# Attention beside a gate product: probabilities turned in their own step, two steps of them kept

## The chip, the cores and the metric

The kernel runs on 1 core of one Trainium2 chip. The metric is the device time of one execution in microseconds (us). Engines are named as in the profile: PE multiplies matrices, PEld is its weight load, DVE, ACT and POOL are the vector, scalar and general engines, SP issues DMAs. Each engine works through its own instructions in the order written; engines meet only through semaphores.

## The reference, cut to what matters

The program computes two transformer blocks on 512 tokens of width 1024. The second has two attentions, each followed by a gated output projection. The change touches only these two:

```python
# fox_attention: 16 heads, causal, with a decay c added to the logits
logits = einsum('bqhd,bkhd->bhqk', qi, k) * scale + ci[..., :, None] - c_k[..., None, :]
p = softmax(where(causal, logits, -inf))
out = einsum('bhqk,bkhd->bqhd', p, v)
# swa_sink_attention: 16 query heads on 4 key heads, a band of 128 tokens, a sink logit per head
probs = softmax(concatenate([logits, sink]))[..., :-1]
out = einsum('bnhgqk,bnkhd->bqhgd', probs, v_band)
# after either
h = h + (o * silu(gate)) @ w_out        # gate = another 1024 columns of the input projection
```

## The kernel before

The attentions of the second block are written by `attend_beside`, once for each engine, and called with FOX and then SWA. Two heads form a unit `m` (8 units). A unit has four steps `i`, one for each tile of 128 queries, the last tile first; steps are numbered `n = 4m + i`, 0 to 31. In FOX a step sees 512, 384, 256 and 128 keys for i = 0, 1, 2, 3; in SWA 256, 256, 256, 128.

A step goes through this chain: PE computes both heads' scores (`scores_of`, L2087 and the masks L2093, L2104); DVE takes the row maxima (`maxima`, L1308); ACT takes the exponentials into a buffer PBS and their sums (`exps`, L798); DVE inverts the sums (`norms`, L1315); POOL multiplies the probabilities by them, in place (L1691); PE turns them (transposes, `turn_p`, L2124) into two PSUM banks; ACT copies one head's bank to PTS (`turned`, L806), DVE the other's (`turned`, L1321); PE multiplies with the values (`values_of`, L2142).

Beside this PE computes the gate: the transposed gate projection has eight tiles of 128 rows, and one tile is spread over the four steps of a unit, six matmuls of 512 columns in each (`part`, L2167). FOX computes one tile and SWA two ahead of step 0 (`lead`), so units 0 to 6 of FOX and 0 to 5 of SWA have gate products, and the last ones have none. All tiles go through one PSUM bank: `part` of step i = 0 waits for ACT's copy of the tile before (`keep_tile`, L825). The weights of later gate tiles and of the output projection are split into two parts in steps i = 1 and 2 of every second unit (`split`; units 1, 3, 5, 7 of FOX and 0, 2, 4, 6 of SWA; L597, L588 or L594 on ACT, then L1001, L990 or L997 on DVE).

In steps i = 2 and 3 PE also transposes the queries and keys of unit m+2 (`turn`, L2153, in SWA keys only for every second unit, L2156 and L2157), directly ahead of the probabilities and into the same two banks; ACT takes their high part (`high`, L818, which waits for DVE's copy of that step's probabilities), DVE the low part (`low`, L1326). `keep` (L829) takes a unit's output from PSUM. At the end of the attention ACT puts SiLU over the gate tiles (`silu`, L841, L875), and the output projection (L1739) waits for the first gated, split tile (L877, L1356).

The order on each engine is written out by hand. PE's before, for step n: scores of step n+1, values of step n-2, turning of step n-1, gate products of step n. `PBS` has three buffers; the exponentials of step n wait until step n-3 is turned.

Of the kernel before, what the change touches and what calls it, by code (L numbers as in the profile page):

```python
# [211 lines left out]
def program(nc, I, out):  # L212
    RUNS = plan()
    LAST = {a: [g for r in RUNS.values() for g in r if g["by"] == a][-1]["freed"] for a in ("act", "dve")}
    with ExitStack() as ctx:
# [6 lines left out]
        def region(name, where, shape, dt=F32, plus=0):  # L222
            return nc.alloc_sbuf_tensor_at(name, [P, *shape], dt, offset=base + at[where] * KB + plus)
# [4 lines left out]
        def sem(name):  # L228
# [20 lines left out]
              region("pt1", "spl", [2, S], plus=28 * KB)]  # L249
        PTS = [region("pts0", "sc", [2, S], plus=24 * KB), region("pts1", "sc", [2, S])]  # L250
        CK = region("ck", "y", [2, S], BF16, plus=12 * KB)
        PBS = {"fox": [region(f"pbf{i}", "y", [2, S], plus=4 * KB * i) for i in range(3)],
               "swa": [region(f"pbs{i}", "qkv", [2, S], plus=6 * KB + 12 * KB * i) for i in range(3)]}
        C3 = region("c3", "sc", [3, S], BF16, plus=8 * KB)
        CREM = region("crem", "sc", [2, S], plus=12 * KB)
        TS = region("ts", "sc", [2, S], plus=8 * KB)
# [79 lines left out]
        def need(a, k, n):  # L336

            return BESIDE[k], n + (BEFORE[k] if a.is_swa else 0)
# [41 lines left out]
        def score_bank(a, s, h):  # L380

            return 4 * (1 - SIDE[a.name]["group"] % 2) + 2 * (s % 2) + h
# [30 lines left out]
        def reach(eng, s, value):  # L413

            if not (isinstance(value, int) and value <= 0):
                eng.wait_ge(s, value)
# [163 lines left out]
        def _(act):  # L580
# [206 lines left out]
            def attend_beside(a):  # L787

                s, g = A[a.name], SIDE[a.name]

                def exps(n):
                    m, i = divmod(n, NT)
                    t = NT - 1 - i
                    reach(act, *need(a, "pt_tr", n - 2))
                    w = a.width(t) + a.sink
                    for h in range(2):
                        act.wait_ge(*need(a, "mx", 2 * n + h + 1))
                        last = act.activation(PBS[a.name][n % 3][:, h, 0:w], PS[:, score_bank(a, n, h), 0:w], ACT.Exp,  # L798
                                              bias=NM[:, m % 2, h, t:t + 1], accum_out=LS[:, m % 2, h, t:t + 1])
                    last.then_inc(s["e"], 1)  # L800

                def turned(n):
                    w = a.width(NT - 1 - n % NT)
                    act.wait_ge(*need(a, "pt_tr", n + 1))
                    reach(act, *need(a, "v", n - 1))
                    act.activation(PTS[0][:, n % 2, 0:w], PS[:, turn_bank(a, PT_BANK), 0:w], ACT.Copy)\  # L806
                       .then_inc(s["pt_a"], 1)

                def high(m, i):
                    if i:  # L810
                        act.wait_ge(*need(a, "tk", a.keys_of(m) + 1))
                    else:
                        act.wait_ge(*need(a, "tq", m + 1))
                    if m >= 2:
                        act.wait_ge(*need(a, "s", 8 * (m - 1)))
                        act.wait_ge(*need(a, "pt_b", NT * (m - 2) + 3 + i))
                    slot = (a.keys_of(m) if i else m) % 2
                    act.activation(turned_to(m, slot, i, HI), turned_at(a, m, i), ACT.Copy).then_inc(s["th"], 1)  # L818

                def keep_tile(k):  # L820
                    if k % 2:
                        act.wait_ge(unit_used, g["unit"] + k // 2 + 1)
                    else:
                        act.wait_ge(*need(a, "tile", k // 2 + 1))
                    act.activation(MX[:, k], PS[:, turn_bank(a, SIDE_BANK)], ACT.Copy).then_inc(s["kept"], 1)  # L825

                def keep(m):
                    act.wait_ge(*need(a, "v", NT * (m + 1)))
                    act.activation(kept_output(m), by_tile(PS[:, turn_bank(a, PV_BANK)]), ACT.Copy)\  # L829
                       .then_inc(s["o"], 1)  # L830

                def split(m, part):
                    if a.split_at(m) is None:
                        return
                    n = g["unit"] + a.split_at(m)
                    act.wait_ge(raw_full[n % 2], 16 * (n // 2 + 1))
                    act.wait_ge(unit_used, n - 1)
                    side_hi(n, part)

                def silu(k):  # L840
                    act.activation(MX[:, k], MX[:, k], ACT.Silu).then_inc(s["silu"], 1)  # L841

                if a.is_fox:
                    act.wait_ge(cum_out, 16)
                    act.wait_ge(x_parked, 16)
                for m, i in a.first_turns():
                    high(m, i)
                for k in range(a.lead):
                    keep_tile(k)
                exps(0)  # L850
                for n in range(a.steps + 2):
                    m, i = divmod(n, NT)
                    if i == 0 and a.tile_at(m - 1) is not None:
                        keep_tile(a.tile_at(m - 1))
                    if n + 1 < a.steps:
                        exps(n + 1)
                    if i == 1 and m:
                        keep(m - 1)
                    if 1 <= n <= a.steps:
                        turned(n - 1)  # L860
                        if a.turn_with(n - 1):
                            high(*a.turn_with(n - 1))
                    if n >= a.steps - 1:
                        silu(2 * (n - a.steps + 1))
                        silu(2 * (n - a.steps + 1) + 1)
                    if i in (1, 2):
                        split(m, i - 1)
            def gated_hi(a):
# [116 lines left out]
        def _(dve):  # L985
# [307 lines left out]
            def attend_beside(a):  # L1293
# [40 lines left out]
                    low(m, i)  # L1334
                maxima(0)
                norms(0)
                for n in range(a.steps + 1):
                    m, i = divmod(n, NT)
                    if n + 1 < a.steps:
                        maxima(n + 1)  # L1340
                    if n >= 1:
                        turned(n - 1)
                    if n + 1 < a.steps:
                        norms(n + 1)
                    if n >= 1 and a.turn_with(n - 1):
                        low(*a.turn_with(n - 1))
                    if i in (1, 2):
                        split(m, i - 1)

# [212 lines left out]
        def _(pool):  # L1562
# [116 lines left out]
            def attend_beside(a):  # L1679
                s = A[a.name]  # L1680
                if a.is_fox:
                    pool.wait_ge(x_parked, 16)
                    pool.memset(CK[:], 0.0).then_inc(ck_zero, 1)
                for n in range(a.steps):
                    m, i = divmod(n, NT)
                    t = NT - 1 - i
                    w = a.width(t)
                    pool.wait_ge(*need(a, "r", n + 1))
                    for h in range(2):
                        p = PBS[a.name][n % 3][:, h, 0:w]  # L1690
                        last = pool.tensor_tensor(p, p, RR[:, m % 2, h, t:t + 1].to_broadcast([P, w]), ALU.mult)  # L1691
                    last.then_inc(s["scaled"], 1)

# [36 lines left out]
        def _(pe):  # L1730
# [339 lines left out]
            def attend_beside(a):  # L2070
# [38 lines left out]
                def turn_p(n):  # L2109
                    t = NT - 1 - n % NT  # L2110
                    pe.wait_ge(*need(a, "scaled", n + 1))
                    reach(pe, *need(a, "pt_a", n))
                    reach(pe, *need(a, "pt_b", n))
                    if n and a.turn_with(n - 1):
                        before, i = a.turn_with(n - 1)
                        if i:
                            pe.wait_ge(*need(a, "kt", a.keys_of(before) + 1))
                        else:
                            pe.wait_ge(*need(a, "qt", before + 1))
                    if a.turn_with(n):  # L2120
                        turn(*a.turn_with(n))
                    for h in range(2):
                        for i in range(a.width(t) // P):
                            last = pe.transpose(PS[:, turn_bank(a, PT_BANK + h), P * i:P * i + P],  # L2124
                                                PBS[a.name][n % 3][:, h, P * i:P * i + P], IDF[:])
                    last.then_inc(s["pt_tr"], 1)

                def values_of(n):
# [61 lines left out]
                pe.wait_ge(freed["act"], last_in[-1]["freed"])  # L2190
                pe.wait_ge(consts, 14)
                scores_of(0)
                for n in range(a.steps + 2):
                    m, i = divmod(n, NT)
                    if n + 1 < a.steps:
                        scores_of(n + 1)
                    if n >= 2:
                        values_of(n - 2)
                    if 1 <= n <= a.steps:
                        turn_p(n - 1)  # L2200
                    part(m, i)

            norm_x(0, None)
            run(RUNS["diff_in"])
# [73 lines left out]
```

## Time and profile before

| | |
|---|---|
| median of three runs | 1901.98 us (1901.42 to 1902.23) |
| profiled execution, its own time | 1901.54 us |
| its span | 1899.7 us |
| PE busy | 1742.6 us (92% of the span) |
| FOX: first scores to the first product of its output projection | 1437.39 to 1566.85 us |
| SWA: the same | 1717.76 to 1846.86 us |
| PE busy in these two stretches | 120.64 of 129.55 us, 109.57 of 129.16 us |

The two attentions take 259 us together. The rest of the program is not touched. A matmul's end is modelled in the profile: the next one starts some 0.1 to 0.3 us ahead of it, so PE's own pace is read from start to start.

### The profile page before, as it was taken

Reading aid. Unit: us, or ns where it says so; the run is one execution under the profiler, and the core shown is the slowest. Engines: PE = TensorE matmul, PEld = TensorE weight load, DVE = VectorE, ACT = ScalarE, POOL = GpSimd, SP = SyncE. Lnnn points to the kernel's source line nnn. Section 1 sums busy time; section 2 is a strip of 40 time slices with the busy share of each in tenths; the row PEclk is TensorE's granted clock in tenths of the full one; section 3 lists DMA queues with packets and bytes.
Section 4 is the critical chain, followed back from the end, with each engine's and each line's share of the span. In section 5 each row is a group of like instructions: output and inputs, shape, how many; then the busy total and the mean of one; then the engine's idle time right before and its main releaser. Section 6 shows DMA issues by size and latency. Waiting matters only on the chain.

```text
span 1899.7 us, 24666 instructions
## 1 busy us (share of the span) xinstructions
PE 1742.6 (92%) x9327; PEld 1354.8 (71%) x9327; DVE 894.4 (47%) x1582; ACT 718.4 (38%) x1568; POOL 367.0 (19%) x498
## 2 busy tenths in 40 slices
PE   6999788999978998998999999989998989888978
PEld 5888557868664554886888888867786767676656
DVE  3782473225445666344343244244644554455552
ACT  3322464122135666323332133133224562434451
POOL 5440242002114564011000000000102330022220
PEclk9999796999987999999999999989999999899979
DMA  6223121422102221432222322332221013220101
GB/s 174 86 92 122 50 73 56 133 89 89 45 12 56 67 58 32 155 104 96 66 90 89 110 89 96 104 111 77 87 82 45 24 36 120 67 89 24 45 23 45
DMA packets 117779, 147.64 MB, mean 78 GB/s; under 512 B 30685, under 2 KB 63733, under 8 KB 117425
## 3 DMA queue, kind: packets, MB, share of 16 engines
q1 hardware_dynamic: 116608, 145.40, 24.0%
q0 software_dynamic: 992, 0.86, 0.4%
q8 instruction: 68, 1.11, 0.2%
q14 instruction: 31, 0.25, 0.0%
q10 hardware_dynamic: 80, 0.02, 0.0%
HBM read 125.24 MB, written 4.24 MB: 68 GB/s over the span
## 4 chain that ended last, share of the span: by engine, by line
PE 81%; ACT 8%; DVE 7%; issue 3%; POOL 1%; DMA 0%; ACTq 0%; DVEq 0%; POOLq 0%
PE ps L1739 57%; PE ps L2167 4%; PE ps L1978 3%; PE ps L2002 2%; ACT pb L740 2%; PE ps L2124 2%; PE ps L2142 2%; PE ps L2087 1%; PE ps L2021 1%; PE ps L2035 1%; DVE qkt L1241 1%; DVE nm L1211 1%; ACT qkt L759 1%; PE ps L1983 1%; PE ps L1876 1%
## 5 line engine op out<-in xcount | busy, mean ns | idle before, releaser
L1739 PE MATMUL ps<-spl,ht 128*128 128x512 f32 x2496 | 584.3, 397 | 26.5 <-DVE xk L1465 8.5
L1739 PEld LDWEIGHTS ps<-spl,ht 128*128 128x128 f32 x2496 | 478.8, 192 | 129.6 <-DVE xk L1465 9.0
L1022 DVE TENSOR_TENSOR spl<-raw,spl 128x1024 fp32r<-128x1024 f32 x180 | 234.7, 1346 | 521.9 <-ACT spl L620 521.9
L620 ACT ACTIVATE spl<-raw 128x1024 fp32r<-128x1024 f32 x180 | 180.5, 1052 | 598.7 <-PE ps L1739 598.7
L1739 PE MATMUL ps<-ht,spl 128*128 128x512 f32 x1152 | 263.9, 391 | 2.0 <-DVE spl L1022 2.0
L1739 PEld LDWEIGHTS ps<-ht,spl 128*128 128x128 f32 x1152 | 217.6, 189 | 48.1 <-issue 2.9
L1739 PE MATMUL ps<-spl,uu 128*128 128x512 f32 x768 | 174.4, 389 | 0.0
L1739 PEld LDWEIGHTS ps<-spl,uu 128*128 128x128 f32 x768 | 144.2, 188 | 29.9
L1636 POOL TENSOR_TENSOR sq<-qkv 128x2048 f32<-128x2048 f32 (+1 forms) x15 | 51.5, 3436 | 372.2 <-ACT qkv L654 357.6
L2167 PE MATMUL ps<-ht,spl 128*128 128x512 f32 x384 | 108.9, 425 | 10.5 <-DVE qkt L1326 5.4
L740 ACT ACTIVATE pb<-ps,nm 128x512 f32<-128x512 f32 (+1 forms) x192 | 99.8, 530 | 45.5 <-DVE nm L1211 45.4
L1672 POOL TENSOR_TENSOR pb<-pb,rg 128x512 f32<-128x512 f32 (+3 forms) x160 | 112.8, 722 | 7.5
L1211 DVE TENSOR_REDUCE nm<-ps 128x1 f32<-128x512 f32 (+1 forms) x192 | 85.2, 485 | 54.4 <-PE ps L1983 54.2
L2167 PEld LDWEIGHTS ps<-ht,spl 128*128 128x128 f32 x384 | 72.6, 201 | 24.8 <-DVE qkt L1326 5.7
L1739 PE MATMUL ps<-ys,spl 128*128 128x512 f32 x384 | 89.2, 395 | 0.0
L1697 POOL MEMSET nws<- 128x2048 f32 x2 | 3.6, 1807 | 440.5 <-PE ps L1739 440.5
L1739 PEld LDWEIGHTS ps<-ys,spl 128*128 128x128 f32 x384 | 73.3, 191 | 15.6 <-issue 0.2
L1978 PE MATMUL ps<-qkt 64*128 64x384 f32 (+3 forms) x576 | 77.4, 377 | 7.2 <-DVE qkt L1241 3.0
L2002 PEld LDWEIGHTS ps<-idf,pb 128*128 128x128 f32 x400 | 44.9, 143 | 36.2 <-issue 29.1
L1691 POOL TENSOR_TENSOR pbf<-pbf,rr 128x512 f32<-128x512 f32 (+3 forms) x64 | 44.7, 721 | 133.6 <-DVE rr L1315 133.6
L1978 PEld LDWEIGHTS ps<-qkt 64*128 64x128 f32 x576 | 47.7, 204 | 28.2 <-issue 23.5
L1308 DVE TENSOR_REDUCE nm<-ps 128x1 f32<-128x257 f32 (+5 forms) x128 | 53.3, 437 | 30.3 <-PE ps L2104 27.7
(292 smaller groups left out, 2060.8 us busy)
## 6 DMA issues: line engine op xcount, KB each, us to landing
raw<-w_in SPq DMA_DIRECT2D x30, 1024.0 KB, 5.2
raw<-w_mlp_up SPq DMA_DIRECT2D x16, 1024.0 KB, 5.2
raw<-w_mlp_down SPq DMA_DIRECT2D x16, 1024.0 KB, 5.0
raw<-w_in_a SPq DMA_DIRECT2D x16, 1024.0 KB, 5.3
stq<-qkv SPq DMA_DIRECT2D x32, 256.0 KB, 2.7
raw<-w_in_b SPq DMA_DIRECT2D x8, 1024.0 KB, 5.4
raw<-w_proj_diff SPq DMA_DIRECT2D x4, 1024.0 KB, 5.2
stq<-qkv SPq DMA_DIRECT2D x32, 128.0 KB, 2.5
```

The lines of the kernel that those rows point to most:

```text
L620: act.activation(SPL[:, n % 2, HI, 2 * k:2 * k + 2], RAW[:, n % 2, 2 * k:2 * k + 2], ACT.Copy).then_inc(hi_done, 1)
L740: last = act.activation(p, PS[:, 2 * (idx % 2) + h, 0:w], ACT.Exp, bias=NM[:, m.slot, h, t:t + 1], accum_out=LS[:, m.slot, h, t:t + 1])
L1022: dve.tensor_tensor(SPL[:, n % 2, LO, 2 * k:2 * k + 2], RAW[:, n % 2, 2 * k:2 * k + 2], SPL[:, n % 2, HI, 2 * k:2 * k + 2].bitcast(F32), A ...
L1211: dve.tensor_reduce(top, bank[:, 0:w], AX.X, ALU.max, negate=True).then_inc(s["mx"], 1)
L1308: dve.tensor_reduce(NM[:, m % 2, h, t:t + 1], bank[:, 0:w + a.sink], AX.X, ALU.max, negate=True)\
L1636: pool.tensor_tensor(SQ[:, :, 0:w], QKV[:, :, col:col + w], QKV[:, :, col:col + w], ALU.mult)\
L1672: last = pool.tensor_tensor(p, p, RG[:, m.slot, h, t:t + 1].to_broadcast([P, w]), ALU.mult)
L1691: last = pool.tensor_tensor(p, p, RR[:, m % 2, h, t:t + 1].to_broadcast([P, w]), ALU.mult)
L1739: last = pe.matmul(PS[:, b0 + b], left[:, x], right[:, y], start=(kt == 0 and i == 0), stop=(kt == UK * g["units"] - 1 and i == 2))
L1978: pe.matmul(PS[:, 2 * (idx % 2) + h, 0:w], QKT[r, m.slot, 0, x, P * t:P * t + P], QKT[r, m.slot, 1, y, P * a.first_key(t):P * t + P], star ...
L2002: last = pe.transpose(bank[:, P * i:P * i + P], PB[:, m.slot, h, o:o + P], IDF[:])
L2167: last = pe.matmul(PS[:, turn_bank(a, SIDE_BANK)], wide(SPL[:, n % 2, x])[:, kt, cols], HT[:, y, kt], start=(kt == 0 and j == 0), stop=(kt ...
```

## The change

Turning moves from the step after into the step itself, behind the gate products, and the value products from two steps after into the next one. There is one closing step less. PBS has two buffers. On ACT and DVE the copies move with the turning; `keep` moves from i = 1 to i = 0, and the SiLUs begin one step number earlier.

```diff
-        PBS = {"fox": [region(f"pbf{i}", "y", [2, S], plus=4 * KB * i) for i in range(3)],
-               "swa": [region(f"pbs{i}", "qkv", [2, S], plus=6 * KB + 12 * KB * i) for i in range(3)]}
+        PBS = {"fox": [region(f"pbf{i}", "y", [2, S], plus=4 * KB * i) for i in range(2)],
+               "swa": [region(f"pbs{i}", "qkv", [2, S], plus=6 * KB + 12 * KB * i) for i in range(2)]}
...
 ACT, exps(n)
-                    reach(act, *need(a, "pt_tr", n - 2))
+                    reach(act, *need(a, "pt_tr", n - 1))
 ACT, loop
-                for n in range(a.steps + 2):
+                for n in range(a.steps + 1):
...
                     if n + 1 < a.steps:
                         exps(n + 1)
-                    if i == 1 and m:
+                    if i == 0 and m:
                         keep(m - 1)
-                    if 1 <= n <= a.steps:
-                        turned(n - 1)
-                        if a.turn_with(n - 1):
-                            high(*a.turn_with(n - 1))
-                    if n >= a.steps - 1:
-                        silu(2 * (n - a.steps + 1))
-                        silu(2 * (n - a.steps + 1) + 1)
+                    if n < a.steps:
+                        turned(n)
+                        if a.turn_with(n):
+                            high(*a.turn_with(n))
+                    if n >= a.steps - 2:
+                        silu(2 * (n - a.steps + 2))
+                        silu(2 * (n - a.steps + 2) + 1)
                     if i in (1, 2):
                         split(m, i - 1)
 DVE, loop
-                for n in range(a.steps + 1):
+                for n in range(a.steps):
...
                         maxima(n + 1)
-                    if n >= 1:
-                        turned(n - 1)
                     if n + 1 < a.steps:
                         norms(n + 1)
-                    if n >= 1 and a.turn_with(n - 1):
-                        low(*a.turn_with(n - 1))
+                    turned(n)
+                    if a.turn_with(n):
+                        low(*a.turn_with(n))
                     if i in (1, 2):
                         split(m, i - 1)
 PE, loop
-                for n in range(a.steps + 2):
+                for n in range(a.steps + 1):
...
                         scores_of(n + 1)
-                    if n >= 2:
-                        values_of(n - 2)
-                    if 1 <= n <= a.steps:
-                        turn_p(n - 1)
+                    if n >= 1:
+                        values_of(n - 1)
                     part(m, i)
+                    if n < a.steps:
+                        turn_p(n)
```

PE in the middle of FOX before, two steps (i = 0 and i = 1 of a unit; pbf is PBS, pts PTS, spl with ht the gate products), as far as the second step's value product, of which the first two rows stand:

```order
L2087 MATMUL ps<-qkt 128x256 x6
L2093 MATMUL ps<-ck,oneb 128x256 x2
L2104 MATMUL ps<-causal,id 128x128 x4
L2142 MATMUL ps<-pts_68,qkv 64x128
L2142 MATMUL ps<-pts_69,qkv 64x128
L2124 MATMUL ps<-idf,pbf_73 128x128 x8
L2167 MATMUL ps<-ht,spl 128x512 x6
L2087 MATMUL ps<-qkt 128x128 x6
L2093 MATMUL ps<-ck,oneb 128x128 x2
L2104 MATMUL ps<-causal,id 128x128 x4
L2142 MATMUL ps<-pts_68,qkv 64x128
L2142 MATMUL ps<-pts_69,qkv 64x128
```

The same place after the change, from the first step's gate products on (lines are one lower throughout):

```order
L2166 MATMUL ps<-ht,spl 128x512 x6
L2123 MATMUL ps<-idf,pbf_71 128x128 x8
L2086 MATMUL ps<-qkt 128x256 x6
L2092 MATMUL ps<-ck,oneb 128x256 x2
L2103 MATMUL ps<-causal,id 128x128 x4
L2141 MATMUL ps<-pts_68,qkv 64x128
L2141 MATMUL ps<-pts_69,qkv 64x128
```

The eight transposes of a 512-key step (x8) stood ahead of the gate products; now they stand behind them, and only the next step's scores stand between them and their own value product.

ACT at the end of FOX before (L588 is the second half of a weight split, L841 SiLU, mx the gate tiles):

```order
L798 ACTIVATE pbf_72,ls<-ps,nm 128x128 x2
L806 ACTIVATE pts_68<-ps 128x384
L588 ACTIVATE spl<-raw 128x1024
L806 ACTIVATE pts_68<-ps 128x256
L841 ACT_TABLE_LOAD
L841 ACTIVATE mx<-mx 128x512 x2
L806 ACTIVATE pts_68<-ps 128x128
```

And after the change:

```order
L798 ACTIVATE pbf_72,ls<-ps,nm 128x128 x2
L806 ACTIVATE pts_68<-ps 128x256
L841 ACT_TABLE_LOAD
L841 ACTIVATE mx<-mx 128x512 x2
L588 ACTIVATE spl<-raw 128x1024
L806 ACTIVATE pts_68<-ps 128x128
```

The table load and the first two SiLUs stood behind the second half of the split; now they stand ahead of it.

## Rows read from the trace of the kernel before

**Rows 1.** Windows: us, busy time (instructions) by engine, granted PE clock, DMA share, GB/s

```profile
1469.00:1485.00 16.00, 16.00 (x143) 12.00 (x142) 7.55 (x19) 8.58 (x28) 5.73 (x9) 1.00 0.17 63
1762.00:1769.00 7.00, 4.52 (x44) 3.36 (x44) 4.14 (x13) 4.56 (x15) 1.83 (x4) 1.00 0.25 69
1769.00:1776.00 7.00, 6.72 (x20) 3.80 (x20) 2.18 (x8) 1.91 (x6) 1.30 (x3) 0.53 0.22 83
```

**Rows 2.** Groups by line, PE, 1437 to 1566.8: busy us, mean ns, idle before, releasers

```profile
L2142 PE MATMUL ps<-pts,qkv 128*64 128x128 f32 x320 | 25.4, 289 | 3.9 <-ACT pts L806 3.3 <-DVE pts L1321 0.6
```

**Rows 3.** The same for PE, 1717 to 1846.8

```profile
L2142 PE MATMUL ps<-pts,qkv 128*64 128x128 f32 x224 | 21.2, 308 | 12.5 <-ACT pts L806 11.2 <-DVE pts L1321 1.2
```

**Rows 4.** PE's timeline, steps of a middle unit of FOX: start, us, instructions [idle before]

```profile
1489.26 0.62 PE L2087 MATMUL ps<-qkt 64*128 64x256 f32 x6
...
1490.05 0.44 PE L2142 MATMUL ps<-pts,qkv 128*64 128x128 f32 x4
1490.42 1.09 PE L2124 MATMUL ps<-idf,pbf 128*128 128x128 f32 x8
1491.27 1.64 PE L2167 MATMUL ps<-ht,spl 128*128 128x512 f32 x6
1492.84 0.55 PE L2087 MATMUL ps<-qkt 64*128 64x128 f32 x6
...
1493.51 1.09 PE L2142 MATMUL ps<-pts,qkv 128*64 128x128 f32 x16
1494.53 0.88 PE L2124 MATMUL ps<-idf,pbf 128*128 128x128 f32 x6
1495.16 1.63 PE L2167 MATMUL ps<-ht,spl 128*128 128x512 f32 x6
1496.72 0.96 PE L2087 MATMUL ps<-qkt 64*128 64x512 f32 x6
...
1497.96 0.88 PE L2142 MATMUL ps<-pts,qkv 128*64 128x128 f32 x12
```

**Rows 5.** DVE's timeline, the same stretch

```profile
1491.55 0.69 DVE L1321 COPY pts<-ps 128x512 f32<-128x512 f32 x1 [0.64 <-PE ps L2124]
...
1497.34 1.22 DVE L1001 TENSOR_TENSOR spl<-raw,spl 128x1024 fp32r<-128x1024 f32 x1 [1.16 <-ACT spl L597]
1498.48 1.28 DVE L1308 TENSOR_REDUCE nm<-ps 128x1 f32<-128x512 f32 x2
```

**Rows 6.** PE's timeline, start and end of FOX

```profile
1443.28 1.09 PE L2124 MATMUL ps<-idf,pbf 128*128 128x128 f32 x8 [1.31 <-POOL pbf L1691]
...
1559.94 1.12 PE L2142 MATMUL ps<-pts,qkv 128*64 128x128 f32 x8 [0.61 <-DVE pts L1321]
...
1566.85 33.48 PE L1739 MATMUL ps<-spl,ht 128*128 128x512 f32 x137 [3.72 <-DVE ht L1356]
```

**Rows 7.** DVE's timeline, end of FOX

```profile
1559.37 0.42 DVE L1321 COPY pts<-ps 128x256 f32<-128x256 f32 x1
```

**Rows 8.** ACT's timeline, the middle unit of FOX

```profile
1496.24 1.06 ACT L597 ACTIVATE spl<-raw 128x1024 fp32r<-128x1024 f32 x1
1499.26 0.69 ACT L798 ACTIVATE pbf<-ps,nm 128x512 f32<-128x512 f32 x1 [1.95 <-DVE nm L1308]
...
1500.86 0.60 ACT L818 ACTIVATE qkt<-ps 128x512 fp32r<-128x512 f32 x1
1501.34 0.62 ACT L825 ACTIVATE mx<-ps 128x512 f32<-128x512 f32 x1
```

**Rows 9.** POOL's timeline, the middle unit of FOX

```profile
1500.98 2.04 POOL L1691 TENSOR_TENSOR pbf<-pbf,rr 128x512 f32<-128x512 f32 x2 [3.97 <-DVE rr L1315]
```

**Rows 10.** ACT's timeline, end of FOX

```profile
1559.77 1.28 ACT L841 ACT_TABLE_LOAD   x1
1561.07 1.15 ACT L841 ACTIVATE mx<-mx 128x512 f32<-128x512 f32 x2
```

**Rows 11.** PE's timeline, unit 2 of SWA

```profile
1769.28 0.27 PE L2156 MATMUL ps<-idf,qkv 128*64 128x128 f32 x1 [0.65 <-DVE qkt L1326]
```

More of the change, by code:

```diff
@@ L797, in exps @@
                         act.wait_ge(*need(a, "mx", 2 * n + h + 1))
-                        last = act.activation(PBS[a.name][n % 3][:, h, 0:w], PS[:, score_bank(a, n, h), 0:w], ACT.Exp,
+                        last = act.activation(PBS[a.name][n % 2][:, h, 0:w], PS[:, score_bank(a, n, h), 0:w], ACT.Exp,
                                               bias=NM[:, m % 2, h, t:t + 1], accum_out=LS[:, m % 2, h, t:t + 1])
@@ L1689, in attend_beside @@
                     for h in range(2):
-                        p = PBS[a.name][n % 3][:, h, 0:w]
+                        p = PBS[a.name][n % 2][:, h, 0:w]
                         last = pool.tensor_tensor(p, p, RR[:, m % 2, h, t:t + 1].to_broadcast([P, w]), ALU.mult)
@@ L2124, in turn_p @@
                             last = pe.transpose(PS[:, turn_bank(a, PT_BANK + h), P * i:P * i + P],
-                                                PBS[a.name][n % 3][:, h, P * i:P * i + P], IDF[:])
+                                                PBS[a.name][n % 2][:, h, P * i:P * i + P], IDF[:])
                     last.then_inc(s["pt_tr"], 1)
```

## The prediction

> **What bounds the kernel now.** I read the windows first, then PE's timeline with what it waits for, then DVE's, ACT's and POOL's over the same microseconds. In the middle of FOX PE is busy for all of 16.00 us at full clock while DVE and ACT work for about half of that and POOL for a third [rows 1]. So there PE's own work sets the pace, and the softmax chain lies wholly under it. At the end of FOX the gate products have run out, and the value products wait for the copies of the turned probabilities: 3.9 us in all, all of it behind the last gate products [rows 2]. In SWA the steps are shorter and the same kind of wait comes to 12.5 us [rows 3]; after such waits (PE busy for 4.52 of 7.00 us) the granted clock fell to 0.53 for the next 7 us, so at 1.2 GHz for nearly all of it [rows 1]. The question is therefore not whether the change takes work from PE (it takes none: the same matmuls) but whether each wait that it brings is still hidden.
>
> **PE's paces.** From start to start [rows 4]: scores of 256 keys 0.79 (1489.26 to 1490.05), of 128 keys 0.67, of 512 keys 1.24; values of 128 keys 0.37, of 512 keys 1.02; the turning of 512 keys 0.85, of 384 keys 0.63; a step's gate products 1.57. For what is not in the rows I interpolate by blocks: scores of 384 keys 1.02, values of 384 and 256 keys 0.81 and 0.59, turning of 256 and 128 keys 0.41 and 0.20, turning four query blocks 0.49. A turning's end lies 0.24 behind the start of what follows (1490.42 + 1.09 against 1491.27), and the copies begin 0.04 after that end [rows 4, 5]. A DVE copy of 512 keys lasts 0.69 [rows 5]; of 256 keys 0.42, and PE went on 0.15 after it ended (1559.37 + 0.42 to 1559.94) [rows 6, 7].
>
> **Two buffers instead of three.** The exponentials of step n+1 now need step n-1 turned. Their scores stand behind that turning on PE, take 0.67 or more, and a maximum follows; the turning is reported 0.28 after PE goes on. Price 0. Without that cover, it would cost the 0.28.
>
> **The wider gap that is left for the softmax.** For a 512-key step the chain is: DVE's first maximum to ACT's first exponential 0.78 (1498.48 to 1499.26) [rows 5, 8], exponential to POOL 1.72, POOL 2.04 [rows 8, 9], and 0.16 for the two ends: 4.7 us after the scores. PE now has between scores and turning: values 0.59, gate 1.57, turns 0.49 + 0.20, scores 1.02, values 0.37, gate 1.57: 5.8 us. Hidden, with 1.1 to spare. At the start there is less in between: before, PE waited 1.31 shown with the scores of step 2 already issued [rows 6]; now these 0.77 us stand behind the wait. **Plus 0.8.**
>
> **The copies lose their cover.** Before, gate products and scores (1.57 and 0.67 to 1.24) lay between a turning and its value product. Now only the scores do. For 512 keys the copy is usable at 0.24 + 0.04 + 0.69 + 0.15 = 1.12 after PE goes on; the scores behind it (256 keys) take 0.78. PE stands 0.34. For 384 keys (copy estimated 0.56) it is 0.99 against 0.67: 0.32. Behind the two narrow steps stand scores of 512 and 384 keys, long enough. That is 0.66 in each of units 0 to 6: **plus 4.6**.
>
> **The gate tile's bank.** The first gate products of a unit wait for ACT's copy of the tile before. ACT's queue now has ahead of it the copy and the high part of the last step, which come after the gate products instead of before them. From the end of the last turning: DVE's copy 0.04 to 0.33, high part until its queue time of 0.48 is over (1500.86 to 1501.34 [rows 8]) at 0.86, the tile's copy 0.62 [rows 8] and 0.05: 1.53. PE arrives at -0.24 + 1.02 + 0.37 = 1.15. **0.38** for units 2, 4, 6 and, with the split's lateness below, 0.66 for units 3, 5, 7's tiles: **plus 3.1**.
>
> **The splits.** In step i = 2 ACT makes its half behind the copy and the high part, and DVE's next maxima stand behind DVE's half. Before this made the maxima start 0.4 late, hidden [rows 5]. Now both halves wait for a turning that comes after the gate products. From the end of that turning: ACT's copy, high part behind DVE's copy, over at 1.0; split 1.06 to 2.05 [rows 8]; DVE's 1.14 (1497.34 to 1498.48 [rows 5]) until 3.2; first exponential at 4.0, both done at 5.4; then DVE inverts and copies the last step's probabilities, usable at 6.0. PE is there at -0.24 + 1.24 + 0.59 + 1.57 + 0.49 + 0.20 + 1.02 = 4.9. So 1.1 in units 1, 3 and 5: **plus 3.4**.
>
> **The end of FOX.** There is one step less, but no gate product covers anything, a split lies in it (unit 7), and its second half now stands on ACT behind the table load and two SiLUs, as the order shows. By the same sums PE waits 0.9, 0.34 and 0.32 in steps 28 to 30 of PE's order, 2.5 for the copy of step 30 (behind DVE's first split half and the last maxima), and for the last copy: from DVE's previous copy, ACT's table load 1.28 and two SiLUs (1.04 of ACT's queue) [rows 10], its split 1.06, DVE's split 1.2, the copy and 0.15: 3.7 of it uncovered. Sum 7.8. The same sum for before gives 5.7, of which the rows show 3.9 as idle behind the modelled ends [rows 2]. **Plus 2.1.** What follows the last value product (keep, SiLUs, first gated tile) is the same chain as before, with its wait of 3.72 [rows 6].
>
> Here the Trainium skill (ScalarE: Activation LUTs, What ACT_TABLE_LOAD costs) has a higher price than the row: a table load of about 1283 ns and a drain of about 1380 ns for each change of set. The row shows 1.28 us and the first SiLU 0.02 later (1559.77 + 1.28 to 1561.07) [rows 10], so no drain behind it; by the page the last term would be 1.4 larger, by the row it stands.
>
> **FOX together**: 0.8 + 4.6 + 3.1 + 3.4 + 2.1 = **14.0**; I take 13.8, since ACT is a little less behind at the very end.
>
> **SWA.** Its scores are shorter (0.66 and 0.61) and steps narrower. The same sums, laid out step by step, give lateness up to unit 5: before 10.9 (the first steps 1.75; at the splits of units 0 and 2 1.6 + 1.5 + 0.7 and 1.4 + 1.5 + 0.7; unit 4 1.5). After: 2.4 at the start, 1.1 of copies in each of units 1, 3 and 5, 3.1 in units 0 and 2 (0.2, 0.25, 1.35, 0.6, 0.7), 1.4 in unit 4: 13.3. Plus 2.4. The wait of 0.65 ahead of the keys' turning [rows 11] vanishes, since gate products stand in between; that is in the sum. In the last two units, with no gate products: 11.0 before and 10.4 after, one step less: minus 0.6, and another 0.6 less because the short end spends less work at the low clock. Then the clock: before, it fell in unit 2 when waits of that unit came close together. Seven microseconds at 0.53 with 6.72 busy hold work of about 4 us at full clock: some 2.7 lost [rows 1]. After the change the waits there are spread over more places (the largest is 1.35), so I take it that it stays up: minus 2.7. **SWA: 2.4 - 0.6 - 0.6 - 2.7 = -1.5.**
>
> **Sum**: 13.8 - 1.5 = 12.3 us. The sum is made against the profiled execution's 1901.54, which lies 0.4 under the median: 1913.8, or 1914.3 against the median. I say **1914**.
>
> **Rivals.**
> 1. *The clock falls in more places* (14%). For it: in SWA it fell after 4.52 busy of 7.00. Against it: unit 0 had nearly the same waits without a fall, and in FOX's split units I get about a quarter idle. If it falls in three FOX units and in both SWA splits, five falls at 2.7 instead of one: +13.5 - 2.7 over the forecast's none, 1914 + 11 = 1925 or so. The Trainium skill (TensorE: Matmul & The Clock Gate, A second HAM failure mode: psum-queue depth-cycling) describes such a kernel: short idles between groups of matmuls, often enough, make the clock swing. The trace shows one such fall, at 1769, and none in the first split unit.
> 2. *Copies are in time* (17%). If a value product can follow a copy sooner than the 0.15 at the end suggests, or ACT's and DVE's queues run earlier than I lay them, then the 4.6 and most of the 3.1 vanish: 1914 - 7 = 1907. Decides: whether the copy of 512 keys is usable within 0.78.
> 3. *Faster* (5%). The closing step is all that counts. Between the last value products before, 2.7 us each at the end of FOX (1557.3 to 1559.9) and as much in SWA; with both gone, the fall at 1769 avoided (2.7) and the keys' wait (0.65 in three units) hidden, 1902 - 10 = 1892; with a part of the copies' waits, 1897. It decides if no wait stands in units 1 to 6 of FOX.
> 4. *No change* (4%): 2 and 3 cancel, 1902.
>
> **How the numbers follow.** Forecast 60%, its own range 1908 to 1921: each of some forty waits is good to 0.1 or 0.2, one fall of the clock may come or go. Faster by over 0.2% (3.8 us, about what a measurement of this kernel tells from no change): rival 3, 0.05. Same: rival 4, 0.04. Slower: 0.91. The range takes in rival 2 and most of the way to rival 1: 1905 to 1923.
>
> **What would show it.** In FOX's middle PE's timeline should show value products with waits of about 0.1 shown (0.34 less the modelled drain of 0.24) released by DVE's pts, waits for mx (L825) at each unit's first gate product, and a unit of 16.7 us without and 18.2 with a split instead of 15.7. At FOX's end a wait of over 3 us ahead of the last value product, with ACT's table load and SiLUs ahead of the split. FOX's stretch should be 143 us instead of 129.6, SWA's 127 to 129. The prediction is wrong if FOX's middle shows PE without waits, if PE waits for POOL's pbf in every step (a chain longer than 5.8), or if the clock falls in FOX's middle.

## The result: 1911.9 against 1901.7 us, 0.6% slower

| | before | changed |
|---|---|---|
| median | 1901.7 us (4 runs, 1899.9 to 1902.23) | 1911.88 us (4 runs, 1911.18 to 1914.52) |
| ratio | | 1.0058, 95% interval 1.0040 to 1.0075 |
| profiled execution, span | 1901.54, 1899.7 us | 1912.05, 1910.2 us |
| FOX: first scores to the first product of its projection | 129.46 us | 141.19 us |
| between FOX and SWA | 150.91 us | 149.83 us |
| SWA: the same | 129.10 us | 128.58 us |

The prediction was 1914, range 1905 to 1923. The loss lies wholly in FOX (+11.7 us); SWA came out 0.5 us shorter, and the stretch between, whose code is the same, 1.1 us shorter.

PE's timeline of the changed kernel in FOX, from the first gate product of unit 1 to that of unit 2 (columns as in [rows 4]; unit 1 has the splits):

```profile
1458.62 1.65 PE L2166 MATMUL ps<-ht,spl 128*128 128x512 f32 x6 [0.22 <-ACT mx L825]
1460.12 1.04 PE L2123 MATMUL ps<-idf,pbf 128*128 128x128 f32 x8
1461.08 0.62 PE L2086 MATMUL ps<-qkt 64*128 64x256 f32 x6
...
1461.98 1.09 PE L2141 MATMUL ps<-pts,qkv 128*64 128x128 f32 x16
...
1464.50 0.82 PE L2123 MATMUL ps<-idf,pbf 128*128 128x128 f32 x6
1465.26 0.55 PE L2086 MATMUL ps<-qkt 64*128 64x128 f32 x6
...
1466.07 0.88 PE L2141 MATMUL ps<-pts,qkv 128*64 128x128 f32 x12
...
1475.47 0.44 PE L2141 MATMUL ps<-pts,qkv 128*64 128x128 f32 x4 [1.00 <-DVE pts L1321]
1476.58 1.66 PE L2166 MATMUL ps<-ht,spl 128*128 128x512 f32 x6 [0.67 <-ACT mx L825]
```

Two kinds of wait are flagged, for the gate tile's copy (mx) and, in a unit with splits, for the last step's copy (pts). A third is not shown as idle: from the turning of 512 keys to its value product there are 1.86 us (1460.12 to 1461.98) where turning and scores alone took 0.85 + 0.79 before [rows 4]. The modelled ends of the matmuls cover it.

DVE's and ACT's timelines of the same unit show the chain behind the wait of 1.00:

```profile
1461.19 0.69 DVE L1321 COPY pts<-ps 128x512 f32<-128x512 f32 x1 [0.39 <-PE ps L2123]
...
1469.44 0.43 DVE L1321 COPY pts<-ps 128x256 f32<-128x256 f32 x1
1470.61 0.69 DVE L1326 TENSOR_TENSOR qkt<-ps,qkt 128x512 fp32r<-128x512 f32 x1 [0.74 <-ACT qkt L818]
1471.56 1.23 DVE L1001 TENSOR_TENSOR spl<-raw,spl 128x1024 fp32r<-128x1024 f32 x1 [0.25 <-ACT spl L597]
1472.70 1.28 DVE L1308 TENSOR_REDUCE nm<-ps 128x1 f32<-128x512 f32 x2
1474.96 0.17 DVE L1315 RECIPROCAL rr<-ls 128x2 f32<-128x2 f32 x1 [0.97 <-ACT pbf L798]
1475.04 0.29 DVE L1321 COPY pts<-ps 128x128 f32<-128x128 f32 x1
```

```profile
1469.98 0.60 ACT L818 ACTIVATE qkt<-ps 128x512 fp32r<-128x512 f32 x1 [0.16 <-DVE pts L1321]
1470.48 1.05 ACT L597 ACTIVATE spl<-raw 128x1024 fp32r<-128x1024 f32 x1
1473.48 0.69 ACT L798 ACTIVATE pbf<-ps,nm 128x512 f32<-128x512 f32 x1 [1.95 <-PE ps L2123]
```

In the order of the steps: the copy of step 2 releases ACT's high part, that its split, that DVE's split; only then come the maxima of the next unit (1472.70; its scores were issued at 1469.33), their exponentials, and behind these on DVE the copy of step 3 (1475.04), for which PE stands.

The end of FOX in the changed kernel, PE and then ACT:

```profile
1570.01 0.66 PE L2141 MATMUL ps<-pts,qkv 128*64 128x128 f32 x8 [2.31 <-DVE pts L1321]
1570.59 0.44 PE L2123 MATMUL ps<-idf,pbf 128*128 128x128 f32 x2
1574.61 0.69 PE L2141 MATMUL ps<-pts,qkv 128*64 128x128 f32 x4 [3.58 <-DVE pts L1321]
```

```profile
1569.62 1.28 ACT L841 ACT_TABLE_LOAD   x1
1570.91 1.15 ACT L841 ACTIVATE mx<-mx 128x512 f32<-128x512 f32 x2
1571.97 1.04 ACT L588 ACTIVATE spl<-raw 128x1024 fp32r<-128x1024 f32 x1
```

DVE in the same place:

```profile
1573.04 1.23 DVE L990 TENSOR_TENSOR spl<-raw,spl 128x1024 fp32r<-128x1024 f32 x1 [3.18 <-ACT spl L588]
1574.18 0.28 DVE L1321 COPY pts<-ps 128x128 f32<-128x128 f32 x1
```

The last copy on DVE waits behind DVE's half of the split, and that behind ACT's, which now comes after the table load and two SiLUs.

By groups of lines (busy us, mean ns, idle before, releasers), PE from 1437.6 to 1578.8 (FOX) of the changed kernel:

```profile
L2166 PE MATMUL ps<-ht,spl 128*128 128x512 f32 x169 | 46.9, 411 | 2.7 <-ACT mx L825 2.7
L2141 PE MATMUL ps<-pts,qkv 128*64 128x128 f32 x320 | 24.8, 283 | 9.8 <-DVE pts L1321 8.9
...
L2123 PE MATMUL ps<-idf,pbf 128*128 128x128 f32 x160 | 23.0, 274 | 3.0 <-POOL pbf L1690 3.0
```

The value products' waits went from 3.9 [rows 2] to 9.8 us, almost all for DVE's copy.

Where FOX's time lies can be read without the modelled ends, from the start of one group of scores to that of another. Unit 0 is here from the scores of step 1 to those of step 5, units 1 to 6 from there to the scores of step 29, the end from there to the projection; the 1.1 us ahead of step 1's scores are the same in all. The lower four kernels are those of the experiments below.

| | unit 0 | units 1 to 6 | end | FOX |
|---|---|---|---|---|
| before | 15.54 | 93.83 | 18.97 | 129.46 |
| changed | 18.14 | 102.39 | 19.53 | 141.19 |
| SiLUs behind the split | 18.11 | 102.48 | 18.25 | 139.95 |
| splits ahead of the copies | 18.13 | 99.81 | 19.09 | 138.15 |
| both repairs | 18.10 | 97.88 | 19.09 | 136.19 |
| turned ahead of the gate products | 21.52 | 98.64 | 19.59 | 140.87 |

At the scores of step 5 the changed order has done one turning and one value product more than the order of before, about 1.3 us by its rows; that work is moved from the end into unit 0. Put back, the changed kernel's 11.7 us are about 1.3 at the start, 8.6 in the middle and 1.9 at the end (an estimate from the table).

### The profile page after: what moved, and what is told of

It is laid out like the page before. It is cut to its first block, busy times and chain, and to the rows that moved or that the text cites. A ratio compares the mean times of both kernels' runs of the same rounds, so it can differ in the third digit from the quotient of the medians.

```text
span 1910.2 us, 24667 instructions
## 1 busy us (share of the span) xinstructions
PE 1745.2 (91%) x9327; PEld 1359.7 (71%) x9327; DVE 896.2 (47%) x1582; ACT 722.3 (38%) x1568; POOL 366.7 (19%) x498
## 4 chain that ended last, share of the span: by engine, by line
PE 80%; ACT 9%; DVE 7%; issue 3%; POOL 1%; DMA 0%; ACTq 0%; DVEq 0%; POOLq 0%
PE ps L1738 57%; PE ps L2166 4%; PE ps L1977 3%; PE ps L2001 2%; ACT pb L740 2%; PE ps L2141 2%; PE ps L2123 2%; PE ps L2020 1%; PE ps L2086 1%; PE ps L2034 1%; DVE qkt L1241 1%; DVE nm L1211 1%; PE ps L1982 1%; ACT qkt L759 1%; PE ps L1875 1%
## 5 line engine op out<-in xcount | busy, mean ns | idle before, releaser
L1738 PEld LDWEIGHTS ps<-ys,spl 128*128 128x128 f32 x384 | 73.5, 192 | 15.7 <-issue 0.2
L2001 PE MATMUL ps<-idf,pb 128*128 128x128 f32 x400 | 64.2, 285 | 0.0
```

What stands on the lines that cost most here:

```text
L1738: last = pe.matmul(PS[:, b0 + b], left[:, x], right[:, y], start=(kt == 0 and i == 0), stop=(kt == UK * g["units"] - 1 and i == 2))
L2001: last = pe.transpose(bank[:, P * i:P * i + P], PB[:, m.slot, h, o:o + P], IDF[:])
```

## The experiments

Stretches are from one profiled execution of each; times are medians of the runs named. The edits are shown against the changed kernel, unless said otherwise.

### Three buffers in the new order

```diff
-        PBS = {"fox": [... for i in range(2)], "swa": [... for i in range(2)]}
+        PBS = {"fox": [... for i in range(3)], "swa": [... for i in range(3)]}
-                    reach(act, *need(a, "pt_tr", n - 1))
+                    reach(act, *need(a, "pt_tr", n - 2))
```
(and the buffer's number `n % 3` instead of `n % 2` on ACT, POOL and PE)

> The changed kernel's order with three probability buffers instead of two, in both attentions. Theory A (the order costs: copies, gate tile's bank, splits, end of FOX): nothing comes back, since the exponentials' scores stand behind the turning on PE; FOX's stretch stays at 141.2 us within 0.5, the time at 1912 within 2. Rival B (the missing third buffer costs): FOX's stretch falls towards 129.5 us and the time towards 1902; anything under 1908 speaks for it. Rival C (falls of the clock cost): no change either, but the cost then has to lie in stretches at 1.2 GHz.

FOX took 141.20 us (141.19 with two), SWA 128.61 (128.58). The one run's 1909.0 us differs through what lies ahead of FOX: there the first scores came at 1434.67 us, in the changed kernel at 1437.69, from the same code. So in the new order the third buffer is worth nothing, and rival B falls. The time missed the expected 1912 within 2 by 1.0 us, for that reason.

### Two buffers in the old order

```diff
-                    reach(act, *need(a, "pt_tr", n - 2))
+                    reach(act, *need(a, "pt_tr", n - 1))
```
(in the kernel before, and both lists with two buffers)

> The order of before, with two probability buffers. Here the turning of step n-1 stands in the same step of PE as the scores of step n+1 and behind them, so the exponentials of n+1 wait for it: their start moves from 0.8 us behind the scores to the end of values and turning, 1 to 2 us. Theory A: by the sums of the prediction this is not hidden at the splits of FOX and in SWA: FOX 129.5 plus 4 to 7, SWA plus 2 to 5, time 1907 to 1913. Rival B as the whole cause would give the same here as the changed kernel, 1912, and a FOX stretch of 141. If the buffers cost nothing in any order: 1902.

1910.3 us (one run), FOX 134.22 and SWA 132.94. The old order needs the third buffer: its absence costs FOX 4.8 us, and in every unit of the middle (16.3 to 16.4 us instead of 15.7), not only at the splits as expected. The new one doesn't need it, and costs 11.7 for other reasons. The two halves of the change can't be priced apart and added.

### SWA alone, FOX alone

```diff
         self.lead, self.run, self.steps = lead, run, NT * units
+        self.back = int(name not in ('swa',))
```
(for the second, 'fox'; where `back` is 1, the loops, the offsets and the number of buffers are as before the change)

> SWA in the new order with two buffers, FOX as before with three. Theory A: FOX's stretch 129.5, SWA's 127 to 130 (in the changed kernel 128.6 against 129.1), time 1899 to 1903. Rival C (the clock decides): a fall of the clock more or less in SWA moves this by 2.7 us either way. If SWA carries a real part of the loss, the time is over 1904.

> FOX in the new order with two buffers, SWA as before with three. Theory A: FOX's stretch 141.2, SWA's 129.1, time 1901.7 plus 10 to 12, 1911 to 1914, nearly the whole loss. If the two attentions share the loss: about 1907.

SWA alone: 1899.1 us (10 runs, 1896.2 to 1904.0) against 1901.2 of before on the same chip, ratio 0.9991 (0.9982 to 1.0001): no difference that can be told. Its SWA stretch was 125.95 us, under the expected 127 to 130. FOX alone: 1908.5 us (6 runs), under the expected 1911 to 1914, ratio 1.0035 (1.0022 to 1.0048), with a FOX stretch of 141.16 as in the changed kernel. So the loss is FOX's. In the profiled execution it is +11.7 in FOX, -1.1 between the two and -3.6 in SWA, which took 125.51 us against 129.10 with the same code as before. That the other five runs are short for the same reason is likely, but they have no trace.

What made SWA shorter is the clock. In unit 2 both executions have the same waits, of 1.36 and 0.65 us. First the kernel before (the wait of 0.65 is in [rows 11]), then this one:

```profile
1767.97 0.66 PE L2142 MATMUL ps<-pts,qkv 128*64 128x128 f32 x8 [1.36 <-ACT pts L806]
...
1769.48 0.69 PE L2157 MATMUL ps<-idf,qkv 128*64 128x128 f32 x2
```

```profile
1780.32 0.66 PE L2147 MATMUL ps<-pts,qkv 128*64 128x128 f32 x8 [1.36 <-ACT pts L807]
1781.62 0.27 PE L2161 MATMUL ps<-idf,qkv 128*64 128x128 f32 x1 [0.65 <-DVE qkt L1328]
1781.82 0.43 PE L2162 MATMUL ps<-idf,qkv 128*64 128x128 f32 x2
```

Behind them the same two transposes take 0.69 us in one and 0.43 in the other: in one execution the clock fell to 1.2 GHz, in the other it stayed at 2.4. The second had its own fall earlier, 20 us after SWA's first scores, and hardly one in the last two units, where before ran some 12 us at the low clock. The fall in unit 2 cost the kernel before 2.8 us (20.57 from the scores of step 13 to those of step 17, against 17.74). The earlier one cost FOX alone 1.5, and its end, from the scores of step 29, was 2.2 shorter (17.99 against 20.23). Together that is the 3.6.

The changed order of SWA has such a pair of times too, and in the traces the case goes with the clock at the moment SWA begins. Here are the last 4 us ahead of SWA's first scores (columns as in [rows 1]), in the kernel before and then in FOX alone, where the second row is the fall 20 us behind them:

```profile
1713.76:1717.76 4.00, 4.00 (x18) 2.96 (x16) 3.17 (x5) 0.00 (x0) 0.00 (x0) 0.86 0.00 0
```

```profile
1724.62:1728.62 4.00, 4.00 (x17) 2.96 (x15) 3.57 (x5) 0.00 (x0) 0.00 (x0) 0.91 0.00 0
1748.62:1752.62 4.00, 4.00 (x14) 2.44 (x15) 0.62 (x3) 1.60 (x6) 0.43 (x1) 0.57 0.15 56
```

All traces whose SWA has the instructions of before or of the changed kernel:

| SWA's stretch | entered at 0.86 or 0.87 | entered at 0.91 |
|---|---|---|
| order of before | 129.10 (before) | 125.51 (FOX alone) |
| changed order | 125.95 (SWA alone), 125.91 (SiLUs behind the split) | 128.58 (changed), 128.61 (three buffers) |

Compared at one entry, the changed order is 3.2 us faster or 3.1 slower. The changed kernel's -0.5 compares one entry with the other and says nothing of the order. What sets the entry, the kernel's FOX or the single execution, is open: no kernel was traced twice, and the order of before has one trace at each entry.

### SiLUs behind the split again

```diff
+                    if i in (1, 2):
+                        split(m, i - 1)
                     if n >= a.steps - 2:
                         silu(2 * (n - a.steps + 2))
                         silu(2 * (n - a.steps + 2) + 1)
-                    if i in (1, 2):
-                        split(m, i - 1)
```

> The changed kernel with the second half of the weight split ahead of the table load and the first two SiLUs on ACT, as before the change. Theory A: the wait ahead of FOX's last value product (3.58 us shown) shrinks by 1.2 to 1.6, FOX's stretch goes from 141.2 to 139.6 to 140.2 us; nothing changes in SWA, where no split lies there. If the table load is not what the last copy waits for: 141.2.

FOX 139.95 us, 1.24 less; the one run took 1908.5 us. The SiLUs' place at the end costs that much. SWA's instructions are the same as in the changed kernel, and its 125.91 us instead of 128.58 are the other entry of the clock (above).

### The splits ahead of the copies

ACT, and likewise DVE behind its `norms`:

```diff
+                    if i in (1, 2):
+                        split(m, i - 1)
                     if n < a.steps:
                         turned(n)
...
-                    if i in (1, 2):
-                        split(m, i - 1)
```

> The changed kernel with the weight splits on ACT and DVE ahead of the copies of their step instead of behind them. Theory A: the waits of 1.0 us for pts (L1321) in FOX's units 1, 3 and 5 vanish and with them the lateness of the gate tiles behind them (0.67 to about 0.25), and at FOX's end the last wait shrinks: FOX 141.2 minus 4 to 6. In SWA the scaled split is 1.7 us, longer than the room ahead of the copies, so the copies come late: SWA plus 2 to 4. If the splits are not the cause of the 1.0 us: FOX within 1 of 141.2.

1911.6 us (one run). FOX 138.15, 3.0 less and not 4 to 6. By the table, 2.6 of it lie in units 1 to 6 and 0.4 at the end: the split stands ahead of the SiLUs too, which alone gave 1.2, but now PE waits for the copies of steps 29 and 30, 2.12 and 2.18 us, behind DVE's two split halves. In the middle PE's timeline shows a new wait in the units with splits:

```profile
1466.56 0.88 PE L2141 MATMUL ps<-pts,qkv 128*64 128x128 f32 x12 [0.68 <-DVE pts L1321]
...
1475.59 1.69 PE L2166 MATMUL ps<-ht,spl 128*128 128x512 f32 x6 [0.26 <-ACT mx L825]
```

The 1.0 and 0.67 are gone, but the copy of the 384-key step now stands behind DVE's split. SWA took 131.09, against 128.58 in the changed kernel, as expected and for the reason given there: DVE's scaled split takes 1.67 us, and the value products' waits for DVE's copies in unit 2 went from 1.19 and 0.42 to 2.34 and 1.03.

### The gate tile's copy ahead of the last copy

```diff
-                    if i == 0 and a.tile_at(m - 1) is not None:
-                        keep_tile(a.tile_at(m - 1))
                     if n + 1 < a.steps:
                         exps(n + 1)
+                    if i == 3 and a.tile_at(m) is not None:
+                        keep_tile(a.tile_at(m))
```

> The changed kernel with ACT's copy of the gate tile ahead of the last step's copy and high part instead of behind them. Theory A: PE's waits for mx (L825), 0.22 to 0.67 in each unit 1 to 6 of FOX (2.7 in sum), vanish: FOX's stretch 141.2 minus 2.2 to 2.8. In SWA the waits of 0.67 vanish too, but copies may come later: between minus 1.5 and plus 0.5. If PE waits for something else there as well: no change.

FOX 139.22, 2.0 less, slightly under the forecast: all six waits for mx went, but waits for ACT's copy came in their place in three units, 1.15 instead of 1.00 and a new one of 0.29. The one run took 1911.2 us, SWA 126.10.

### Both repairs

The splits ahead of the copies and the gate tile's copy ahead of the last copy, both edits as above.

> The changed kernel with two repairs together: the splits ahead of the copies (which also puts the second half ahead of the SiLUs), and the gate tile's copy ahead of the last step's copy. Theory A: FOX's stretch was 138.15 with the first alone; the waits of about 0.25 for mx (L825) in six units go too, 136.5 to 137.2. What is left over the 129.5 of before is then the start, the end and the copies with their uncovered share; if the repairs only move the waits, FOX stays at 138.

FOX 136.19 us, a little better than expected, with none of the waits for mx; SWA 132.86, the time 1913.2 (one run). With both repairs FOX is still 6.7 us over before.

### Turned in its own step, ahead of the gate products

```diff
-                    part(m, i)
                     if n < a.steps:
                         turn_p(n)
+                    part(m, i)
```

> The turning stays in its own step, with two buffers, but stands ahead of the gate products. The copies then have gate products and scores as cover again, while the softmax chain loses one gate product (1.57 us) of its own. Theory A: the waits for pts and mx in the middle of FOX vanish, waits for pbf of 0.4 to 1.0 come at every unit's first step, 3.6 at the start; FOX 141.2 minus 5 to 6, still 5 to 7 over the 129.5 of before; SWA minus 3 to 5 against the changed kernel in the same state of the clock, so at or below before. Time 1902 to 1905. Rival D (turning in its own step costs by itself, wherever it stands): FOX stays near 141 and SWA near 128.

1907.5 us (10 runs), ratio 1.0032 (1.0021 to 1.0044), over the expected 1902 to 1905. FOX took 140.87, not 135 to 136. Its timeline:

```profile
1441.36 1.97 PE L2123 MATMUL ps<-idf,pbf 128*128 128x128 f32 x8 [3.71 <-POOL pbf L1690]
1442.98 2.91 PE L2166 MATMUL ps<-ht,spl 128*128 128x512 f32 x6
...
1460.04 1.09 PE L2123 MATMUL ps<-idf,pbf 128*128 128x128 f32 x8 [0.48 <-POOL pbf L1690]
...
1476.95 1.10 PE L2123 MATMUL ps<-idf,pbf 128*128 128x128 f32 x8 [1.13 <-POOL pbf L1690]
```

The waits in the middle are as expected: none for pts or mx, 0.48 or 1.13 for pbf once a unit. Units take 16.27 and 16.91 us instead of 16.47 and 17.96 in the changed kernel. At the start came something that wasn't expected: after the wait of 3.71 the same eight transposes took 1.97 instead of 1.09 us and the gate products 2.91 instead of 1.65, the low clock. The first unit took 2.4 us more than a later one without a split (18.68 against 16.27). By the table units 1 to 6 took 3.8 us less than in the changed kernel and unit 0 3.4 more.

By its total, 140.87, FOX stayed near 141, which is what rival D had said; by its parts the place within the step does decide in FOX's middle. The expected total was wrong by two things, the clock at the start and a term for the copies that was too large to begin with (below). SWA took 125.81 us, no less than the changed order at its better entry (125.91 and 125.95), so for SWA this run doesn't decide against rival D.

### SWA alone, ahead of the gate products, FOX as before

As SWA alone above, with SWA's turning ahead of the gate products.

> FOX as before with three buffers; SWA turned in its own step with two buffers, but ahead of the gate products. Theory A: FOX's stretch 129.5; SWA's 122.5 to 124 us where the clock falls only at its end, 125 to 127 with a fall in unit 0 or 2, against 125.5 and 129.1 in the order of before: time 1.5 to 3 us under before, 1898 to 1900.5. If SWA's waits are only moved: the same as before within 1 us.

1898.5 us (12 runs, 1896.3 to 1901.1) against 1901.0 (17 runs) on the same chip: ratio 0.9984, interval 0.9974 to 0.9994. It is 2.5 us faster than before, somewhat more than the measurement is uncertain. Its profiled SWA stretch was 125.90 us, within the expected 125 to 127 for a fall in unit 0, which it had: from 4 to 12 us after its first scores. That is no less than SWA alone with the turning behind the gate products (125.95, without an early fall), and the intervals of the two ratios overlap. So this kernel is shown to be a little faster than before; that the place ahead of the gate products is what brings it is not shown.

## Why the prediction was right, point by point

The forecast of 1914 was 2 us too high, and part of that nearness is luck. The sum had +13.8 for FOX, -1.5 for SWA and nothing for the rest; the profiled executions show +11.7, -0.5 and -0.8 (+0.3 ahead of FOX, -1.1 between). FOX's term was right in its mechanism, in the places of the waits and mostly in their sizes. SWA's term came out near because the two executions happened to meet the clock differently.

**PE sets the pace, and no work is taken from it**: right. PE's busy time rose by 2.6 us only (1742.6 to 1745.2); the rest is waits.

**Two buffers, price 0**: right in the new order (three buffers: 141.20 against 141.19).

**Start, +0.8**: right. PE's wait went from 1.31 [rows 6] to 2.12:

```profile
1443.58 1.09 PE L2123 MATMUL ps<-idf,pbf 128*128 128x128 f32 x8 [2.12 <-POOL pbf L1690]
```

**The wider chain is hidden**: right in units 0 to 6; no wait for pbf until step 28 (0.87, 0.9 forecast).

**Copies, +4.6**: the mechanism was right, the size too large: with the gate tile's wait taken away a unit without splits still took 16.15 us instead of 15.71 before, so the copies cost some 0.44 in a unit and not 0.66. Turning to value product was laid at 1.97 us for 512 keys and 1.62 for 384; the rows after show 1.86 and 1.57. Two details are behind it: PE went on 0.10 after DVE's copy ended (1461.19 + 0.69 to 1461.98), not 0.15, and the turning itself takes longer when scores follow it (0.96 for 512 keys, 0.76 for 384, against 0.85 and 0.63 ahead of gate products [rows 4]), while gate products followed by a turning take 1.50 instead of 1.57. Ahead of the gate products again, the turning of 512 keys took 0.85 (1460.04 to 1460.89 in the profile of that experiment). A unit without splits took 16.47 us (first gate product to first gate product) and not the 16.7 forecast, one with splits 17.96 and not 18.2; a quarter of a microsecond in each of seven units is most of the difference between 13.8 and 11.7 for FOX. The sign named in the prediction, small waits for pts ahead of these value products, didn't come: nothing is flagged there, and the gap shows only from start to start.

**Gate tile's bank, 0.38 and 0.66**: 0.22 to 0.25 and 0.67; 2.7 in sum instead of 3.1. Moving the tile's copy gave 2.0 back.

**Splits, +3.4**: three waits of 1.0. Right, and their cause is the chain shown above: with the splits ahead of the copies all three are gone.

**End of FOX**: waits of 2.31 and 3.58 shown, 2.5 and 3.7 forecast. The table load's place was worth 1.2 (SiLUs behind the split again). By the table the end costs about 1.9 in all, 2.1 forecast. The row has the load at 1.28 us with the first SiLU 0.01 behind it (0.02 before). By this row the term stood rightly: the drain of about 1380 ns that the Trainium skill adds to a load (ScalarE: Activation LUTs, What ACT_TABLE_LOAD costs) is not in either trace.

**SWA, -1.5**: -0.5, with a wrong step in it: "I take it that it stays up: minus 2.7". In unit 2 it did stay up, and the size was right (2.8, above). But it fell in the first steps instead, after waits at the start that had grown from 0.87 and 0.61 to one of 2.33 us:

```profile
1728.70:1735.00 6.30, 3.97 (x43) 2.99 (x44) 2.58 (x11) 4.12 (x11) 1.44 (x3) 1.00 0.01 3
1735.00:1740.00 5.00, 5.00 (x38) 3.73 (x36) 1.72 (x7) 1.46 (x6) 2.11 (x4) 0.66 0.00 0
```

That cost 1.5 us (21.52 from SWA's first scores to those of step 5, against 20.00 in SWA alone, where it didn't fall after the same wait, 2.34). FOX alone shows that the old order need not fall in unit 2 either. So the term should have been a spread of about 3 us on both sides and not a gain. Two sums of the prediction don't come out as stated. The lateness of SWA before, by its own terms, is 10.65 and not 10.9. Five falls are 13.5 over a forecast with none, so the first rival's time would be about 1927 and not 1925.

Of the rivals, the second (copies in time, 1907) had part of the truth in its sizes, but not by its own test: the copy of 512 keys was usable 0.90 us after PE went on (1461.08 to 1461.98) and not within 0.78. The first (falls of the clock in FOX's middle) did not come: FOX's granted clock was 0.97 as before.

FOX with both repairs is 6.7 us over before. By the table and the waits this is, as an estimate, 0.8 at the start, 2.0 in three waits of 0.68 for the 384-key copy behind DVE's split, some 0.4 in each of six units for the uncovered copies, and about 1.5 at the end.

What stays open is what sets the clock at which SWA is entered, and with it whether any order of SWA is better than the other by more than that; and where the 2.5 us of the fastest kernel lie.

## What to carry to other kernels

A step that is moved closer to its consumer can save latency only where nothing covers it, and in the full stretch it takes cover from the transfer between them. Here FOX's middle lost 8.6 us, and its end, where the saving was to be, lost 1.9. Before moving one, lay out for each pair on the path what stands between producer and consumer, and for each engine what now stands ahead of its half. Here the order of the queues on ACT and DVE (a weight split, a table load, a tile's copy) made 5.0 of the 11.7 us, which a reordering gave back; the rest is cover that the move itself takes away, from the copies and, at the start, from the softmax chain. A buffer count has no price of its own: the third buffer was worth nothing in one order and, in FOX, 4.8 us in the other.

## What the runs showed of the hardware that was not expected

In the traces TensorE's clock fell or stayed up for the same instructions and the same waits: in the order of before, SWA took 129.10 us at a mean of 0.91 and 125.51 at 0.98, in the changed order 128.58 at 0.91 and 125.95 at 0.96. In six traces the case went with the clock of the last 4 us ahead of SWA, 0.86 or 0.87 against 0.91, and the order that gained at one entry lost at the other. An order of steps that leaves short waits should therefore be compared at the same entry, or over many executions.

The stretch ahead of FOX, identical in all kernels, ended between 1434.67 and 1440.06 us, and the 17 runs of before on one chip spread from 1898.7 to 1906.7. The stretches of a profile, FOX's 129.40 to 129.46 in three kernels and 141.16 to 141.20 in three others, tell far more than a single run's time.

Eight transposes took 0.85 us of PE's queue ahead of matmuls of 512 columns and 0.96 ahead of matmuls of 256. A duration from start to start, read ahead of one neighbour, is not that ahead of another; why was not looked into.
